# Delta rule of a DeltaNet block: the joins of six chunks in nine common steps, with the work between them placed by hand

## The chip, the cores and the metric

The kernel runs on one core of a Trainium2 chip. It is one program that issues instructions to five engines by hand: TensorE (PE in the profile, its weight loads PEld), VectorE (DVE), ScalarE (ACT), GpSimd (POOL) and SyncE (SP, which issues the weight loads from HBM). The engines wait for each other through semaphores. The metric is device time in microseconds (us) from start to end of one execution.

## The reference, cut to what matters

The block is a DeltaNet layer, an attention layer and a third layer with three attention branches and a feed-forward part. The change touches only the DeltaNet layer. There, for 16 value heads in both directions of time, tokens are cut into chunks, and each chunk needs the inverse of a triangular matrix:

```python
a = jnp.where(strict, jnp.einsum('bhncd,bhnsd->bhncs', kb, kc) * decay, 0.0)
t_inv = lax.linalg.triangular_solve(eye + a, jnp.broadcast_to(eye, a.shape),
                                    left_side=True, lower=True, unit_diagonal=True)
u = jnp.einsum('bhncs,bhnse->bhnce', t_inv, vb)
def step(s, xs):                              # the scan over chunks
    v_new = u_i - jnp.einsum('bhcd,bhde->bhce', w_i, s)
    o = jnp.einsum('bhcd,bhde->bhce', qd_i, s) + jnp.einsum('bhcs,bhse->bhce', qk_i, v_new)
    s = s * gl_i[..., None, None] + jnp.einsum('bhcd,bhce->bhde', kd_i, v_new)
...
o = rms_norm(o, o_norm_g)
return (o * jax.nn.silu(z)) @ w_out           # the gate
```

q, k and v come from a projection `u @ w_in`, a five-tap convolution over time and a silu; z from another projection. All is float32.

## The kernel before

The kernel uses 6 chunks of 128 tokens (768 in all) and goes over the 16 heads in 8 passes `j` of two heads; each pass also prepares the next one, `k = j + 1`. The order of work is one list, the generator `dn_order`. Every engine's program walks through the same list and issues its own part of each entry, in that order, so that the list sets the order on PE, DVE, ACT, POOL and SP alike. A pass has three stages:

- **Substitution.** The 16x16 diagonal blocks of all matrices go to HBM (`blocks_out`, issued by SP) and come back in another layout (`blocks_in`). DVE inverts them in 15 steps (`solve`). SP sends the inverses out and back (`inverses_out`) into `Yf`. Beside this PE runs the projection of the next pass: `proj(k, n, part)`, with `n` one of four groups of 128 columns (q, k and two v heads) and `part` one of four pieces of two contraction steps each, so 16 pieces `p[0]` to `p[15]`. When a group is done ACT copies it from PSUM to `raw`, and DVE runs its five taps (`conv(k, n, q)`). The five taps of the first group stand between the `solve` steps in DVE's queue, `conv(k, 0, 0)` behind the third step, and so the fourth step is not issued before this group is in `raw`.
- **Joins.** The inverse is put together from blocks of 16 to 32, 64 and 128 by nine steps (the table `JOINS`: x, p, y for size 16 and 32; x, w, y for 64), each on each of the six chunks. PE does 8 (sizes 16 and 32) or 4 small matmuls per chunk and step, and ACT or DVE copies each product out of PSUM before the next step of that chunk. Chunks 0 to 2 and 3 to 5 are two gangs, the second one step behind the first. Between these half steps stand larger pieces for PE: the rest of the projection, 24 pieces of the gate's projection `z`, the norms' sums (`norm`) and transposes (`turn`). The function `with_dense` cuts this list into runs, which are spread evenly over the 18 half steps.
- **Scan.** Six steps over the chunks in both directions, with the next pass's decay and Gram matrices between them. Then the outputs of both directions are summed.

The gate of pass j-1 ends in pass j: `sum_sq` (mean square, DVE and ACT), `gate_o` (two multiplications over 128x1536, DVE), `finish` (12 transposes on PE, a copy by ACT and a store). Before, `zg` (the silu of z, with two table loads on ACT, a multiplication on POOL) is the last entry ahead of the scan of its own pass.

SP's program hangs its weight loads on entries of the same list. A projection slab (2 MB, `in_w_dn`) goes to one slot of a ring of two, a gate slab (1 MB, `in_w_z`) to the other; each load waits until PE has read the slab that it replaces. SP issues in order, and a wait holds all that stands behind it:

```python
elif what == "proj" and which[1:] == [3, 3]:
    ahead += 1
    fetch(ahead)                    # the gate slab of pass k
elif what == "zg" and which[0] < 7:
    ahead += 1
    fetch(ahead)                    # the projection slab of the pass after the next
elif what == "gram" and which[1] == 1:
    blocks_out(which[0], 0, 0, 2)
elif what == "blocks":
    blocks_out(which[0], 1, 2, 6)
    blocks_in(*which)
elif what == "solved":
    inverses_out(*which)
```

`proj` waits at its part 0 for the slab. In the profile L995 and L996 are `proj`, L1032 is `z`, L1004 and L1005 `norm`, L1013 `turn`, L1074 to L1133 the join steps (L1074 x, L1084 p, L1096 y; L1109, L1121, L1133 those of size 64), L1145 to L1185 the scan, L1196 `finish`; L2283 and L2286 `conv`, L2333 and L2336 `solve`, L2412 and L2415 `gate_o` (all DVE); L1782 and L1783 `zg` (ACT); L791 `fetch`, L800 `blocks_out`, L808 `blocks_in`, L813 to L821 `inverses_out` (SP).

## Time and profile before

| | us |
|---|---|
| median of 3 runs (lowest to highest) | 3429.66 (3426.16 to 3442.43) |
| profiled execution | 3430.6 |
| its span, first to last instruction | 3428.6 |
| PE busy | 3031.3 (88%) |
| DVE busy | 1322.4 (39%) |
| ACT busy | 982.0 (29%) |

The profile is one execution. Start times count from its first instruction. A timeline row is a start time, a duration, engine, line and operation, what it writes and reads, and a count of merged instructions (a float32 matmul shows as two); in brackets stands how long the engine had been idle, and what it waited for. The joins of pass 3 begin at 663.56 us and those of pass 7 at 1282.31 us, so that a pass takes 154.7 us. The granted TensorE clock over the span is 0.961 of full speed, which is 2.4 GHz.

### The profile page before, as it was taken

The page shows a single profiled execution, that of the slowest core. Times are in us where ns is not written, and L with a number is a line of the kernel's source. Part 1 is how long each engine was busy: PE and PEld are TensorE (multiplying, and loading weights), DVE is VectorE, ACT ScalarE, POOL GpSimd, SP SyncE. Part 2 cuts the span into 40 slices and gives each one's busy share as a digit, 9 for nine tenths or more (in the row PEclk, how much of TensorE's full clock was granted, in tenths as well). Part 3 has the DMA queues.
Part 4 walks back from the last instruction along what each step waited for, and adds up shares of the span by engine and source line. Part 5 has one row for each costly group of instructions (what it writes and reads, how often), then busy time and mean ns, then how long its engine had stood idle before and what let it go on. Part 6 is the DMA issues. An engine that isn't in the chain of part 4 may idle for free.

```text
span 3428.6 us, 38158 instructions
## 1 busy us (share of the span) xinstructions
PE 3031.3 (88%) x15910; PEld 1898.8 (55%) x15910; DVE 1322.4 (39%) x2862; ACT 982.0 (29%) x2457; POOL 64.4 (2%) x52
## 2 busy tenths in 40 slices
PE   7798888888898869797999979999989989799998
PEld 3466667676666647464555433545454433388743
DVE  2346364636455453442322123322235210377601
ACT  1325435353535344001223122221124310212200
POOL 0000000000000000000000000000000000000000
PEclk9799999999999989899999999999999999899999
DMA  4101100010101011710100011111221012022211
GB/s 182 38 9 51 43 19 38 19 39 19 39 19 50 23 65 50 314 51 31 49 25 25 31 46 74 50 50 53 83 74 39 35 74 88 35 99 74 76 68 41
DMA packets 75644, 195.99 MB, mean 57 GB/s; under 512 B 56048, under 2 KB 60144, under 8 KB 64080
## 3 DMA queue, kind: packets, MB, share of 16 engines
q1 hardware_dynamic: 70064, 173.73, 14.0%
q10 hardware_dynamic: 5408, 19.83, 1.5%
q8 instruction: 125, 2.05, 0.2%
q14 instruction: 47, 0.39, 0.0%
HBM read 182.00 MB, written 11.53 MB: 56 GB/s over the span
## 4 chain that ended last, share of the span: by engine, by line
PE 75%; DVE 10%; ACT 9%; DMA 3%; issue 2%; SPq 1%; DVEq 0%
PE ps L939 12%; PE ps L1619 7%; PE ps L1032 5%; PE ps L1556 5%; PE ps L1434 5%; PE ps L1251 3%; ACT arena L1657 3%; PE ps L1566 2%; PE ps L995 2%; PE ps L1438 2%; PE ps L1318 2%; PE ps L929 2%; PE ps L1333 2%; PE ps L1252 2%; PE ps L1074 2%
## 5 line engine op out<-in xcount | busy, mean ns | idle before, releaser
L1656 ACT ACTIVATE arena<-ps 64x64 f32<-64x64 f32 (+9 forms) x952 | 314.5, 358 | 1101.2 <-PE ps L939 354.7
L939 PE MATMUL ps<-arena 128*128 128x512 f32 (+1 forms) x976 | 420.4, 590 | 46.5 <-DVE arena L2232 15.2
L939 PEld LDWEIGHTS ps<-arena 128*128 128x128 f32 x976 | 187.6, 194 | 273.5 <-issue 229.9
L995 PE MATMUL ps<-arena 128*128 128x512 f32 x512 | 265.2, 599 | 1.7 <-DVE arena L2232 1.7
L1619 PE MATMUL ps<-arena 128*128 128x256 f32 x1176 | 254.5, 378 | 0.0
L1619 PEld LDWEIGHTS ps<-arena 128*128 128x128 f32 x1176 | 222.2, 189 | 32.6 <-issue 0.5
L1032 PE MATMUL ps<-arena 128*128 128x256 f32 x768 | 205.4, 404 | 15.0 <-DVE arena L2304 8.7
L1657 ACT ACTIVATE arena<-ps,arena 128x128 f32<-128x128 f32 x544 | 158.4, 368 | 140.8 <-PE ps L1057 48.3
L1556 PE MATMUL ps<-arena 128*128 128x512 f32 x384 | 173.2, 603 | 20.3 <-issue 20.3
L1434 PE MATMUL ps<-arena 128*128 128x512 f32 x384 | 179.8, 596 | 5.1 <-ACT arena L1988 3.2
L996 PEld LDWEIGHTS ps<-arena 128*128 128x128 f32 x512 | 97.0, 189 | 124.4 <-issue 124.4
L1032 PEld LDWEIGHTS ps<-arena 128*128 128x128 f32 x768 | 138.7, 194 | 39.1 <-DVE arena L2304 9.5
L996 PE MATMUL ps<-arena 128*128 128x256 f32 x512 | 152.7, 380 | 0.0
L2551 DVE SCALAR_TENSOR_TENSOR arena<-arena 128x512 f32<-128x512 f32 x45 | 30.5, 748 | 307.7 <-ACT arena L1672 307.7
L1251 PE MATMUL ps<-arena 128*128 128x512 f32 x256 | 133.1, 601 | 16.8 <-DMA arena<-scratch 16.8
L1556 PEld LDWEIGHTS ps<-arena 128*128 128x128 f32 x384 | 73.2, 194 | 110.1 <-issue 110.1
L2286 DVE SCALAR_TENSOR_TENSOR arena<-arena 128x770 f32<-128x770 f32 x128 | 130.2, 1017 | 2.9
L1318 PEld LDWEIGHTS ps<-arena 128*128 128x128 f32 x728 | 99.9, 193 | 47.8 <-issue 20.4
L1665 ACT ACTIVATE arena<-arena 128x512 f32<-128x512 f32 (+2 forms) x61 | 37.4, 628 | 294.0 <-DVE arena L2471 195.2
L2510 DVE SCALAR_TENSOR_TENSOR arena<-ps,arena 128x128 f32<-128x128 f32 (+2 forms) x80 | 31.3, 392 | 210.1 <-PE ps L1532 139.7
L1318 PE MATMUL ps<-arena 128*128 128x128 f32 x728 | 103.5, 277 | 8.5 <-DVE arena L2520 8.4
L995 PEld LDWEIGHTS ps<-arena 128*128 128x128 f32 x512 | 95.6, 191 | 14.9 <-issue 1.8
(295 smaller groups left out, 4200.8 us busy)
## 6 DMA issues: line engine op xcount, KB each, us to landing
arena<-in_ada_w SPq DMA_DIRECT2D x12, 2048.0 KB, 17.4
arena<-in_w_up SPq DMA_DIRECT2D x11, 2048.0 KB, 7.8
arena<-in_w_dil SPq DMA_DIRECT2D x9, 2048.0 KB, 7.6
arena<-in_w_dn SPq DMA_DIRECT2D x8, 2048.0 KB, 9.7
arena<-in_w_gate SPq DMA_DIRECT2D x6, 2048.0 KB, 12.5
arena<-in_w_down SPq DMA_DIRECT2D x8, 1408.0 KB, 6.1
arena<-in_att_in SPq DMA_DIRECT2D x5, 2048.0 KB, 8.0
arena<-in_w_z SPq DMA_DIRECT2D x8, 1024.0 KB, 5.0
```

Of the source, the lines that this page charges most:

```text
L939: m = e.matmul(out, w[:, (k * m_tiles + x) * 128:(k * m_tiles + x) * 128 + 128], src(k), start=k == 0, stop=k == nk - 1)
L995: e.matmul(ps[:, b1, :], w, uT[:, k * T_ALL + 256:(k + 1) * T_ALL], start=k == 0, stop=k == 7)
L996: m = e.matmul(ps[:, b2, 0:256], w, uT[:, k * T_ALL:k * T_ALL + 256], start=k == 0, stop=k == 7)
L1032: m = e.matmul(ps[:, b, (c % 2) * 256:(c % 2) * 256 + 256], uT[:, k * T_ALL + c * 128:k * T_ALL + c * 128 + 128], wv[:, k, :], start=k == ...
L1251: e.matmul(ps[:, b, :], lhsT, s[:, 256:768], start=k == 0, stop=k == 15)
L1318: m = e.matmul(psf[:, b * 512 + c * 128:b * 512 + c * 128 + 128], P[:, c * 128:c * 128 + 128], diag[lane], start=True, stop=True)
L1434: m = e.matmul(ps[:, b, :], w[:, (4 * k + n) * 128:(4 * k + n) * 128 + 128], hk(k), start=k == 0, stop=k == 7)
L1556: m = e.matmul(ps[:, b, :], w[:, k * 512 + x * 128:k * 512 + x * 128 + 128], hk(k), start=k == 0, stop=k == 7)
L1619: m = e.matmul(ps[:, b, 0:256], left[:, k], right[:, k], start=k == 0, stop=k == 3)
L1656: return e.activation(out, x, ACT.Copy)
L1657: return e.activation(out, x, ACT.Copy, scale=scale)
L2286: e.scalar_tensor_tensor(cv[n], r[:, q:q + 770], cw[:, q:q + 1], cv[n], MUL, ADD).then_inc(*(mark("tap", j, n, q) if q < 4 else mark("conv ...
```

## The change

- The joins are no longer two gangs. Each of the nine steps is issued for all six chunks, and behind each step stands a list written by hand (`behind`).
- Each chunk has its own buffer `joined` (six per size in place of three), so `join_p` no longer waits for the `y` step of chunk c - 3. The loads that fill them at the start double from 6 to 12, 128 KB each.
- `p[14]` and the first two taps of `conv(k, 2)` move ahead of the first join step.
- `zg(j)` moves out of the joins of pass j to the substitution of pass j + 1, between `p[2]` and `p[3]`; in pass 7 it stays in the joins. `gate_o` moves from ahead of the `solve` steps to behind step 8, `finish` from behind step 7 to behind step 12.
- The PSUM banks of the projection groups are exchanged (`PROJ`).
- SP's program is not edited, but its `fetch` at `zg` moves with the entry.

```diff
--- before.py
+++ after.py
@@ -248,20 +248,6 @@
 JOINS = [(what, size) for size in (16, 32) for what in ("x", "p", "y")] + [("x", 64), ("w", 64), ("y", 64)]
 
 
-
-DENSE = ("proj", "z", "norm", "turn", "mod_k")
-
-
-def with_dense(slices):
-
-    runs = []
-    for s in slices:
-        if s[0] in DENSE or not runs:
-            runs.append([])
-        runs[-1].append(s)
-    return runs
-
-
 def dn_order():
 
 
@@ -278,6 +264,9 @@
 
     def gate(j, i, banks=(0, 1)):
         return [("z", j, c, part, banks[i % 2]) for c in (2 * i, 2 * i + 1) for part in range(4)]
+
+    def beside(one, other):
+        return [x for both in itertools.zip_longest(one, other) for x in both if x]
 
     def norms(j, n):
         return [("norm_sq", j, n), ("norm", j, n), ("norm_x", j, n), ("turn", j, n)]
@@ -311,48 +300,54 @@
             yield next(z)
     for j in range(8):
         k = j + 1
+
         if j < 7:
             p = project(k)
-
-            taps = [*conv(k, 2, 2, 5), *conv(k, 3)]
-            z = gate(j, 0) if j else []
-            rest = [p[14], *conv(k, 2, 0, 2), p[15], *(x for pair in itertools.zip_longest(taps, z) for x in pair if x),
-                    ("silu", k), ("norm_sq", k, 0), *gate(j, 1), ("norm", k, 0), ("norm_x", k, 0), ("norm_sq", k, 1),
-                    ("turn", k, 0), *gate(j, 2), ("norm", k, 1), ("norm_x", k, 1), ("turn", k, 1), ("zg", j)]
+            t = [*conv(k, 2, 2, 5), *conv(k, 3)]
+            z1, z2 = gate(j, 1), gate(j, 2)
+            if j:
+                z0 = gate(j, 0)
+                behind = [[p[15]], beside(t[:4], z0[:4]), beside(t[4:], z0[4:]), z1]
+            else:
+                behind = [[p[15]], beside(t[:4], z1[:3]), beside(t[4:], z1[3:5]), z1[5:]]
+            behind[2] += [("silu", k), ("norm_sq", k, 0)]
+            behind += [[("norm", k, 0), ("norm_x", k, 0), ("norm_sq", k, 1)], [("turn", k, 0), *z2[:3]], z2[3:],
+                       [("norm", k, 1), ("norm_x", k, 1)], [("turn", k, 1)]]
         else:
             p = [("mod_k", n, x) for n in (4, 5) for x in range(8)]
-            rest = [*p[14:], *gate(7, 0), *gate(7, 1), *gate(7, 2), ("zg", 7)]
+            z0, z1, z2 = (gate(7, i) for i in range(3))
+            behind = [[p[15]], z0[:4], z0[4:], z1[:4], z1[4:], z2[:3], z2[3:6], [*z2[6:], ("zg", 7)], []]
         yield "clean", j
         yield "blocks", j
         if j:
             yield "sum_sq", j - 1
         yield from p[:3]
         if j:
-            yield "gate_o", j - 1
+            yield "zg", j - 1
         yield p[3]
-        beside = {3: 4, 5: 5, 8: 6, 10: 7, 12: 8, 14: 9}
+        early = {3: 4, 5: 5, 8: 6, 10: 7, 12: 8, 14: 9}
         for i in range(1, 16):
             yield "solve", j, i
-            if i in beside:
-                yield p[beside[i]]
+            if i in early:
+                yield p[early[i]]
                 if j < 7 and i < 14:
-                    yield "conv", k, 0, beside[i] - 4
-            if i == 7 and j:
+                    yield "conv", k, 0, early[i] - 4
+            if i == 8 and j:
+                yield "gate_o", j - 1
+            if i == 12 and j:
                 yield "finish", j - 1
         yield "solved", j
         yield p[10]
         if j < 7:
             yield from conv(k, 1)
         yield from p[11:14]
-        runs, done = with_dense(rest), 0
-        steps = [(gang, at) for step in range(len(JOINS) + 1) for gang, at in ((range(3), step), (range(3, 6), step - 1))
-                 if 0 <= at < len(JOINS)]
-        for i, (gang, at) in enumerate(steps):
-            for c in gang:
-                yield (*JOINS[at], j, c)
-            now = len(runs) * (i + 1) // len(steps)
-            yield from itertools.chain(*runs[done:now])
-            done = now
+        if j < 7:
+            yield from conv(k, 2, 0, 2)
+        yield p[14]
+        for (what, size), more in zip(JOINS, behind):
+            for c in range(6):
+                yield what, size, j, c
+            yield from more
         also = {s: [] for s in range(6)}
         if j < 7:
             for s, c in enumerate((0, 3, 4, 2, 5)):
@@ -505,7 +500,7 @@
 
 
         Ab, XT, tmp16 = take(768), take(768), take(450)
-        joined = {size: [take(256) for _ in range(3)] for size in (16, 32)}
+        joined = {size: [take(256) for _ in range(6)] for size in (16, 32)}
         XL = [rr, vn, vd, qs, Ab[:, 0:512], Sst]
         XW = [oB[:, c * 256:c * 256 + 256] for c in range(6)]
 
@@ -677,7 +672,7 @@
             return x.rearrange("p (m f l) -> p m f l", m=4, f=4)
 
 
-        PROJ, GRAM = ((0, 1), (2, 3), (6, 7), (0, 1)), (0, 1, 1, 3, 0, 3)
+        PROJ, GRAM = ((6, 7), (0, 1), (2, 3), (0, 1)), (0, 1, 1, 3, 0, 3)
 
         LEFT = (1, 1, 5, 4, 4, 5)
 
@@ -1094,7 +1089,7 @@
                 for u in range(4):
                     for U in UPPER:
                         m = e.matmul(ps[U, b, u * 32:u * 32 + 32].rearrange("p (b t) -> p b t", t=size),
-                                     un64(joined[size][c % 3][U], u), blocks_of(quadrant(Yf, c, u, U, U), size, u % 2, 1),
+                                     un64(joined[size][c][U], u), blocks_of(quadrant(Yf, c, u, U, U), size, u % 2, 1),
                                      start=True, stop=True)
                 m.then_inc(*mark("inv_pe", j, c, "y", size))
                 leave_banks(("inv_act", j, c, "y", size), b)
@@ -1692,7 +1687,7 @@
             e.dma_start(expa, D["a_log"].partition_broadcast(128)).then_inc(*landed("in_alog"))
             e.dma_start(onorm, D["o_norm_g"].partition_broadcast(128)).then_inc(*landed("in_onorm"))
             for i, size in enumerate((16, 32)):
-                for n in range(3):
+                for n in range(6):
                     e.dma_start(joined[size][n], D["join"][i]).then_inc(*landed(f"in_joins{size}", n))
 
 
@@ -2342,12 +2337,9 @@
 
             def join_p(size, j, c):
                 e.wait_ge(*at("inv_pe", j, c, "p", size))
-                if c < 3:
-                    e.wait_ge(*at(f"in_joins{size}", 2))
-                else:
-                    e.wait_ge(*at("inv_pe", j, c - 3, "y", size))
+                e.wait_ge(*at(f"in_joins{size}", 5))
                 for d in range(2):
-                    m = e.tensor_tensor(both(joined[size][c % 3], size, d, 0), narrow(2 + c, size, d), partners(size, d), MUL)
+                    m = e.tensor_tensor(both(joined[size][c], size, d, 0), narrow(2 + c, size, d), partners(size, d), MUL)
                 m.then_inc(*mark("inv_dve", j, c, "p", size))
 
             def halves_x(j, c):
```

SyncE, from the end of one pass's inverses to those of the next (98 rows in both). Before, with L791 the weight loads, L800 `blocks_out`, L808 `blocks_in`, L813 to L821 the inverses:

```order
L821 DMA arena<-blocks 16x24x16 x8
L791 DMA arena<-in_w_z 128x2048
L791 DMA arena<-in_w_dn 128x4096
L800 DMA blocks<-arena 16x8x16 x8
L800 DMA blocks<-arena 16x16x16 x8
L808 DMA arena<-blocks 96x256 x2
L813 DMA blocks<-arena 96x256
```

In the changed kernel the same lines are numbered five lower:

```order
L816 DMA arena<-blocks 16x24x16 x8
L786 DMA arena<-in_w_z 128x2048
L795 DMA blocks<-arena 16x8x16 x8
L795 DMA blocks<-arena 16x16x16 x8
L803 DMA arena<-blocks 96x256 x2
L786 DMA arena<-in_w_dn 128x4096
L808 DMA blocks<-arena 96x256
```

The 2 MB slab `in_w_dn` now stands behind both `blocks_out` and `blocks_in`. It does so for the slabs 2 to 7, and once more for `in_ada_w` in pass 7.

TensorE, the first half of the joins of pass 1. Before:

```order
L1074 MATMUL ps<-arena 64x64 x24
L995 MATMUL ps<-arena 128x512
L996 MATMUL ps<-arena 128x256
L995 MATMUL ps<-arena 128x512
L996 MATMUL ps<-arena 128x256
L1084 MATMUL ps<-arena 64x32 x24
L995 MATMUL ps<-arena 128x512
L996 MATMUL ps<-arena 128x256
L995 MATMUL ps<-arena 128x512
L996 MATMUL ps<-arena 128x256
L1074 MATMUL ps<-arena 64x64 x24
L1032 MATMUL ps<-arena 128x256 x2
```

In the changed kernel, from the last piece ahead of the joins (L990 and L991 are `proj`, L1069, L1079 and L1091 the steps x, p and y, L1027 `z`):

```order
L991 MATMUL ps<-arena 128x256
L1069 MATMUL ps<-arena 64x64 x48
L990 MATMUL ps<-arena 128x512
L991 MATMUL ps<-arena 128x256
L990 MATMUL ps<-arena 128x512
L991 MATMUL ps<-arena 128x256
L1079 MATMUL ps<-arena 64x32 x48
L1027 MATMUL ps<-arena 128x256 x8
L1091 MATMUL ps<-arena 64x32 x48
L1027 MATMUL ps<-arena 128x256 x8
L1069 MATMUL ps<-arena 64x64 x48
L1027 MATMUL ps<-arena 128x256 x16
```

Half steps of 24 small matmuls became steps of 48, and one piece of two L995 and two L996 left the joins.

VectorE, in the substitution of pass 1, around `solve` step 8. Before:

```order
L2336 TENSOR_REDUCE arena<-arena 96x2x8
L2286 SCALAR_TENSOR_TENSOR arena<-arena 128x770
L2333 TENSOR_TENSOR arena<-arena 96x162
L2336 TENSOR_REDUCE arena<-arena 96x2x9
L2333 TENSOR_TENSOR arena<-arena 96x200
```

In the changed kernel:

```order
L2331 TENSOR_REDUCE arena<-arena 96x2x8
L2281 SCALAR_TENSOR_TENSOR arena<-arena 128x770
L2404 TENSOR_TENSOR arena<-arena 128x1536
L2407 TENSOR_TENSOR arena<-arena 128x1536
L2328 TENSOR_TENSOR arena<-arena 96x162
```

The two multiplications of `gate_o` moved from ahead of the first step to the middle of the chain of steps.

## Rows read from the trace of the kernel before

**Rows 1.** SP's issues, passes 2 and 3 (start, duration, engine, line, operation, count)

```profile
569.72 0.43 SPq L791 DMA_DIRECT2D arena<-in_w_dn  x1
603.58 27.29 SPq L800 DMA_DIRECT2D blocks<-arena  x16
632.33 0.78 SPq L808 DMA_DIRECT2D arena<-blocks  x2
654.98 0.30 SPq L813 DMA_DIRECT2D blocks<-arena  x1
```

**Rows 2.** PE's timeline, substitution of pass 3

```profile
624.60 1.02 PE L995 MATMUL ps<-arena 128*128 128x512 f32 x2
...
634.49 0.59 PE L996 MATMUL ps<-arena 128*128 128x256 f32 x2
...
640.08 1.47 PE L1196 MATMUL ps<-arena 128*128 128x128 f32 x12
...
661.60 0.59 PE L996 MATMUL ps<-arena 128*128 128x256 f32 x2
663.56 1.61 PE L1074 MATMUL ps<-arena 64*64 64x64 f32 x48 [1.36 <-DMA arena<-blocks]
```

**Rows 3.** DVE's timeline, the same stretch

```profile
635.38 1.76 DVE L2412 TENSOR_TENSOR arena<-arena 128x1536 f32<-128x1536 f32 x1 [2.69 <-ACT arena L1877]
637.25 1.76 DVE L2415 TENSOR_TENSOR arena<-arena 128x1536 f32<-128x1536 f32 x1
...
639.99 0.61 DVE L2283 TENSOR_SCALAR arena<-arena 128x770 f32<-128x770 f32 x1
...
654.33 0.62 DVE L2336 TENSOR_REDUCE arena<-arena 96x30 f32<-96x450 f32 x1
```

**Rows 4.** ACT's timeline, the same stretch

```profile
634.28 0.64 ACT L1656 ACTIVATE arena<-arena 96x256 f32<-96x256 f32 x1 [3.37 <-DMA arena<-blocks]
...
635.26 0.85 ACT L1656 ACTIVATE arena<-ps 128x512 f32<-128x512 f32 x2
```

**Rows 5.** DMA issues by line: KB each, median us from issue to landing

```profile
arena<-in_w_dil SPq DMA_DIRECT2D x9, 2048.0 KB, 7.6
arena<-in_w_dn SPq DMA_DIRECT2D x8, 2048.0 KB, 9.7
...
arena<-in_w_down SPq DMA_DIRECT2D x8, 1408.0 KB, 6.1
```

**Rows 6.** PE's timeline, first work after an idle stretch

```profile
54.23 2.04 PE L995 MATMUL ps<-arena 128*128 128x512 f32 x2 [1.70 <-DVE arena L2232]
...
1261.62 2.82 PE L1196 MATMUL ps<-arena 128*128 128x128 f32 x12 [9.08 <-DVE arena L2415]
```

**Rows 7.** busy time in the joins of pass 3 (span, engines, PEclk, DMA)

```profile
core 0: us, PE busy (x) PEld busy (x) DVE busy (x) ACT busy (x) POOL busy (x), PEclk, DMA share, GB/s
663.56:728.79 65.23, 59.49 (x852) 46.16 (x853) 19.22 (x48) 27.05 (x91) 0.00 (x0) 0.97 0.05 17
```

**Rows 8.** PE's timeline, joins and first scan step of pass 3

```profile
674.34 1.61 PE L1074 MATMUL ps<-arena 64*64 64x64 f32 x48
675.88 2.00 PE L1032 MATMUL ps<-arena 128*128 128x256 f32 x8
...
708.14 0.88 PE L1013 MATMUL ps<-arena 128*128 128x128 f32 x6 [0.99 <-ACT arena L1761]
...
711.85 1.38 PE L1032 MATMUL ps<-arena 128*128 128x256 f32 x4 [1.31 <-DVE arena L2304]
...
728.79 1.06 PE L1164 MATMUL ps<-arena 128*128 128x128 f32 x8
...
733.69 2.08 PE L1185 MATMUL ps<-arena 128*128 128x128 f32 x8 [1.40 <-ACT arena L1657]
```

**Rows 9.** ACT's timeline, start of the scan of pass 3

```profile
728.92 1.28 ACT L1782 ACT_TABLE_LOAD   x1
...
733.01 1.14 ACT L1657 ACTIVATE arena<-ps,arena 128x128 f32<-128x128 f32 x4
```

## The prediction

> **What bounds the kernel now.** I read the busy shares first: PE 88%, DVE 39%, ACT 29%. A pass is bound by PE's queue, so I went through PE's timeline of one pass and asked at each gap what it waited for. In the substitution PE has no gap: it starts the next projection at 624.60 and is at it until 662.19 (661.60 + 0.59), `finish` of 1.47 included; then it waits 1.36 for the inverses to come back [rows 2]. DVE's chain of `solve` steps runs beside it and ends at 654.95 [rows 3], 8.6 before the first join step. Both sides of this stage end within 2 us of each other, so a delay of either moves the joins. In the joins PE is busy 59.5 of 65.2 us at a granted clock of 0.97 [rows 7], with waits of about 1 us each [rows 8]. At the start of the scan PE waits 1.40 for ACT, which was busy with the table loads and the silu of `zg` [rows 8, 9].
>
> Then I read SP's queue, since the order listing shows a 2 MB load moved past other entries. Before, the slab `in_w_dn` is issued at 569.72, 55 us ahead of its use in pass 3 at 624.60, and its landing (9.7 us, behind a gate slab that shares the engines) is hidden [rows 1, 2, 5]. `blocks_out` ends at 630.87 (603.58 + 27.29) and `blocks_in` is issued from 632.33 to 633.11 [rows 1]: 8.5 us after PE has begun the projection that needs the slab.
>
> **The change part by part, for a middle pass, in the times of pass 3.**
>
> *The slab.* In the changed kernel it is issued behind `blocks_in`, at 633.1. Six slabs (2 to 7) are so placed. Nothing else held it up: its slot was free since the joins. What stands behind it on SP is only the inverses' trip at 654.98 [rows 1]. A 2 MB load that does not share the engines takes 7.6 (the median of nine); 6.1 for 1.4 MB and 9.7 for the shared one are the ends [rows 5]. I take 7.7: landing at 640.8. PE's queue has nothing else ahead of `proj` part 0, so PE stands from 624.6 to 640.8: **+16.2 us** (14.6 to 18.2).
>
> The rate can also be had from the Trainium skill, "DMA: Bandwidth & Descriptors", section "Anatomy of one DMA": 2.0 us fixed plus bytes at 436 GB/s. For 2.10 MB that is an estimate of 6.8 us, 0.9 under what I take; six slabs would cost 5 us less, 3468 in place of 3473. The rows of 7.6 decide here.
>
> *The clock.* After a long stretch of little work TensorE came back at 1.2 GHz: the first pair took 2.04 against 1.02, and after 9.08 us of idling `finish` took 2.82 against 1.47 [rows 2, 6]. Pass 3 goes straight from scan to projection and has no such start. I add **+1.5** (0 to 3).
>
> *What follows the late start.* PE: 640.8 + 1.5 + 37.6 (624.60 to 662.19) = 679.9, and `p[14]`, a fourth of the 10.3 that four pieces take (624.60 to 634.49 + 0.59 [rows 2]), makes it 682.5. DVE: `solve` 1 to 3 run early, but `conv(k, 0, 0)` behind them needs group 0 out of PSUM: 640.8 + 1.5 + 10.5 plus ACT's two copies of 0.85 [rows 4] = 653.6. From that conv to the end of the chain it was 15.0 (639.99 to 654.95), and `gate_o` now stands inside the chain, 3.6 (635.38 to 639.01) [rows 3]: 672.2, and 8.6 for the trip: 680.8. So PE is the later by 1.7 and the joins begin at 682.5, 18.9 after 663.56. Of this 2.6 is `p[14]`, which the joins no longer hold: net **+16.3**. Without the late slab `gate_o`'s move would cost nothing, as it was ahead of the chain anyway; `zg` on ACT (4.1 from table load to the next instruction [rows 9]) falls where ACT waits for PE, in either case. POOL's part of it has 14 us until `gate_o`.
>
> *The joins.* Six chunks in step leave between a copy and its use the rest of the step (1.6 per three chunks) and a piece from `behind` (2.0 to 8 us of `z` at 2.00 for two pieces [rows 8]). That can remove the 5.7 of idle time and the loss by the clock, 0.03 x 65.2 = 2.0 [rows 7]. Where two edges stay uncovered I charge a wait of about 1 us, the size of those at 708.14 and 711.85 [rows 8]: `turn(k, 0)` must be copied out by DVE before `z` may have the bank, and the last `norm` puts ACT's Ln and Exp ahead of its copies of the final step. That is 2.1. Sum: -5.7 - 2.0 + 2.1 = **-5.6** (-7.7 to 0). That work is not less is plain from the order: the same number of matmuls, in longer rows. The buffers per chunk remove a wait (chunk c - 3's `y`) which the gangs had always behind them; alone 0.
>
> *The scan.* With `zg` gone ACT's copy can come at DVE's product, not at 733.01: the wait of 1.40 goes, and the slow matmuls behind it (eight of 128x128 take 2.08 there and 1.06 at 728.79) come back in part [rows 8, 9]: **-2.0** (-3 to 0).
>
> *Passes 0 and 7.* In pass 0 the slab in question was loaded at the start, so only gains count: -5.6 - 2.0, and about 1.4 more since it has fewer pieces to cover waits with before: -9. In pass 7 the late load is wanted only in the second half of the `mod_k` pieces, while PE waits for DVE anyway (9.08 idle at 1261.62 [rows 6]), and `zg(7)` still stands ahead of the scan: -1.
>
> *The start.* Six more loads of 128 KB on ACT's queue, long before the joins use them: 0 (up to 1). The exchanged banks: group 0 now needs banks 6 and 7, which the last scan step empties before its own output step, and group 2 uses 2 and 3, which the first join step wants after `p[12]` to `p[14]`: 0.
>
> Per middle pass: 16.3 - 5.6 - 2.0 = +8.7. Six of them: +52.2. With -9 and -1 the sum is +42. Against the profiled execution of 3430.6 that is 3473; the median of the runs shown, 3429.66, lies 0.9 lower, which I ignore.
>
> **The rivals.**
>
> *A, the forecast:* 3473, own range 3455 to 3495.
>
> *B, the joins give nothing back.* ACT has 24 copies in a `y` step of six chunks and, behind the first of them, the silu of q, k and v with its own table loads; DVE has eight taps and `norm_sq` ahead of its six copies. Steps of six put a whole batch behind these where the gangs had half. For it: ACT is 27 us busy in the joins [rows 7]. Against: 3 to 8 us of `z` stand behind just these steps. Its price is 5.6 in each of seven passes (+39) on 3473: 3512, and with the slab at 9.7 us (+12) 3524.
>
> *C, a cheaper slab.* 6.1 us to landing and no slow start of PE: 3.1 less in six passes, 3454; with joins that get all 7.7 back, 3440.
>
> *D, the other side: the slab is not late.* If PE met the slab in time, only the gains would stay: -7.6 in six passes, -9 and -1, together -56, so 3375. This is decided at one point: a landing before about 627, or other work in PE's queue for 16 us. For it speaks only that SP's earlier waits might end sooner, since `blocks_out` waits for DVE's last products; against it, those products are made at the very end of the scan (SP's `blocks_out` ends at 630.87, after PE's last scan work), and the trip itself is unchanged. A part of it, in which gains reach 16.3 per middle pass, would need more than all idle time of the joins, the slow clock and the scan's wait together (5.7 + 2.0 + 3 = 10.7).
>
> **How the numbers follow.** A 0.62, B 0.20, C 0.13, D 0.03, something unseen 0.02 that leaves the time about where it is. A measurement of this kernel can tell 0.5% (17 us) from no change. A, B and most of C are slower by more than that; the lower end of C and the unseen one are "same", 0.05; D is faster, 0.03; slower 0.92. The range from 3445 to 3520 leaves out D, the low end of C and the high end of B.
>
> **What the changed profile would show.** In passes 1 to 6 the first L990 of a projection stands behind a wait of about 16 us for a DMA from `in_w_dn`, and its first rows take twice their time; in pass 0 it does not. SP's timeline has the slab right behind L803. DVE waits about 15 us for ACT between `solve` 3 and the first tap. The distance from the first join step to the first scan step falls from 65.2 to about 57, of which 2.6 is `p[14]`. The wait of L1180 in scan step 0 is gone in passes 0 to 6. If the slab's wait is under 10 us, the size of the first term is wrong; if the distance in the joins stays above 61, B holds.

## The result: 1.2% slower, as the sum had it, and the profile after

Medians of four runs each on one chip: the changed kernel 3475.74 us (3466.38 to 3477.2), the kernel before 3429.68 (3426.16 to 3442.43). The ratio is 1.0122 [1.009, 1.0153]; the forecast was 3473, slower. The profiled run of the changed kernel is its fastest: 3466.38, with a span of 3464.6, 36.0 above the span before. The rows below are from it; their line numbers are the old ones less 5 (L990 and L991 `proj`, L1027 `z`, L1069, L1079 and L1091 the join steps x, p and y).

SP's timeline in pass 3, beside [rows 1]:

```profile
628.69 3.79 SPq L795 DMA_DIRECT2D blocks<-arena  x8
633.97 0.78 SPq L803 DMA_DIRECT2D arena<-blocks  x2
634.79 0.43 SPq L786 DMA_DIRECT2D arena<-in_w_dn  x1
674.47 0.30 SPq L808 DMA_DIRECT2D blocks<-arena  x1
```

The slab is issued right behind `blocks_in`. PE's timeline from its arrival, beside [rows 2]:

```profile
642.53 2.07 PE L990 MATMUL ps<-arena 128*128 128x512 f32 x2 [16.15 <-DMA arena<-in_w_dn]
644.40 1.06 PE L991 MATMUL ps<-arena 128*128 128x256 f32 x2
645.25 1.54 PE L990 MATMUL ps<-arena 128*128 128x512 f32 x2
646.63 0.60 PE L991 MATMUL ps<-arena 128*128 128x256 f32 x2
647.06 1.02 PE L990 MATMUL ps<-arena 128*128 128x512 f32 x2
```

PE stands 16.15 us, and starts at half speed. That this is the path shows in the chain of waits from 626 to 690, where the load itself is one piece:

```profile
634.79 7.69 DMA arena<-in_w_dn
642.53 2.07 PE ps L990 x2
```

The list of waits from 300 to 1300 (total us, times, longest) has it six times:

```profile
DVE arena L2278 <- ACT arena L1651: 110.6, 6, 19.0
PEld ps L990 <- DMA arena<-in_w_dn: 97.5, 6, 16.4
PE ps L990 <- DMA arena<-in_w_dn: 96.4, 6, 16.2
```

Next, what else ran under that wait: ACT's timeline, then DVE's, beside [rows 3, 4]:

```profile
636.96 1.28 ACT L1777 ACT_TABLE_LOAD   x1
638.25 1.48 ACT L1777 ACTIVATE arena<-arena 128x1536 f32<-128x1536 f32 x1
639.75 1.28 ACT L1778 ACT_TABLE_LOAD   x1
655.00 0.87 ACT L1651 ACTIVATE arena<-ps 128x512 f32<-128x512 f32 x2 [13.96 <-PE ps L991]
```

```profile
655.91 0.62 DVE L2278 TENSOR_SCALAR arena<-arena 128x770 f32<-128x770 f32 x1 [18.15 <-ACT arena L1651]
660.98 1.75 DVE L2404 TENSOR_TENSOR arena<-arena 128x1536 f32<-128x1536 f32 x1
662.83 1.76 DVE L2407 TENSOR_TENSOR arena<-arena 128x1536 f32<-128x1536 f32 x1
673.82 0.62 DVE L2331 TENSOR_REDUCE arena<-arena 96x30 f32<-96x450 f32 x1
```

`zg` is over at 641.03 and ACT then idles for 13.96 us, and `gate_o` (L2404, L2407) stands in DVE's chain, which ends at 674.44; PE reaches the joins at 684.59, without a wait there. The joins of pass 3, beside [rows 7, 8]: first their whole stretch (length, then PE, PEld, DVE, ACT, POOL busy, PE's clock, DMA share, GB/s), then rows of PE's timeline.

```profile
684.59:738.36 53.77, 51.50 (x846) 43.55 (x845) 20.73 (x50) 25.23 (x86) 0.00 (x0) 1.00 0.06 21
```

```profile
684.59 3.01 PE L1069 MATMUL ps<-arena 64*64 64x64 f32 x96
687.53 1.12 PE L990 MATMUL ps<-arena 128*128 128x512 f32 x2
...
693.23 3.73 PE L1027 MATMUL ps<-arena 128*128 128x256 f32 x16
696.89 2.99 PE L1091 MATMUL ps<-arena 64*64 64x32 f32 x96
...
706.42 7.20 PE L1027 MATMUL ps<-arena 128*128 128x256 f32 x32
713.55 2.99 PE L1079 MATMUL ps<-arena 64*64 64x32 f32 x96
...
722.80 2.87 PE L1027 MATMUL ps<-arena 128*128 128x256 f32 x12 [1.05 <-DVE arena L2299]
725.60 1.61 PE L1104 MATMUL ps<-arena 64*64 64x64 f32 x48
727.15 4.60 PE L1027 MATMUL ps<-arena 128*128 128x256 f32 x20
...
738.36 0.68 PE L1159 MATMUL ps<-arena 128*128 128x128 f32 x4 [1.22 <-ACT arena L1651]
739.43 0.71 PE L1159 MATMUL ps<-arena 128*128 128x128 f32 x4 [0.39 <-ACT arena L1651]
...
741.19 1.05 PE L1180 MATMUL ps<-arena 128*128 128x128 f32 x8
```

65.2 us have become 53.8. The two waits left are those the forecast charged: `z` behind `turn(k, 0)` (1.05), and ACT's late copies at the edge to the scan (1.22). The wait of 1.40 at the old L1185 [rows 8] is gone.

The ledger of the two profiled runs, from the starts of these stages in all passes:

| stage | before | after | difference |
|---|---|---|---|
| wait for the slab, passes 1 to 6 | 0 | 96.4 | +96.4 |
| projection's first row to the joins, passes 1 to 6 | 235.3 | 254.7 | +19.4 (15.5 of it `p[14]`, which left the joins) |
| joins, passes 1 to 6 | 63.7 to 65.2 each | 53.8 each | -61.1 |
| joins, pass 0 | 59.1 | 46.8 | -12.3 |
| scan, passes 0 to 5 | 52.2 mean | 50.0 mean | -13.1 |
| the rest (start, scan 6 with pass 7's substitution, tail) | | | +6.7 |
| span | 3428.6 | 3464.6 | +36.0 |

The medians differ by 46, ten more. The other three runs of the changed kernel took 3475 to 3477 at a mean granted clock of 0.942 to 0.943, the profiled one 3466 at 0.945. The scan is the stage that varies most: 47.5 to 54.9 us from pass to pass, longer where the granted clock in it is 0.87 to 0.90. What makes the clock drop in some scans stays open; no term of the sum below 10 us can be read from totals alone, and I compare stages.

### The profile page after: what moved, and what is told of

Same layout as the page of the kernel before. It is cut to its first block, busy times and chain, and to the rows that moved or that the text cites. A ratio compares the mean times of both kernels' runs of the same rounds, so it can differ in the third digit from the quotient of the medians.

```text
span 3464.6 us, 38189 instructions
## 1 busy us (share of the span) xinstructions
PE 3019.5 (87%) x15910; PEld 1905.0 (55%) x15910; DVE 1326.0 (38%) x2862; ACT 981.4 (28%) x2457; POOL 64.4 (2%) x52
## 3 DMA queue, kind: packets, MB, share of 16 engines
q8 instruction: 125, 2.05, 0.2%
## 4 chain that ended last, share of the span: by engine, by line
PE 81%; DVE 7%; ACT 7%; DMA 3%; issue 1%; SPq 1%; DVEq 0%; ACTq 0%
PE ps L934 12%; PE ps L1614 7%; PE ps L990 7%; PE ps L1027 5%; PE ps L1551 5%; PE ps L1429 5%; PE ps L991 3%; PE ps L1246 3%; ACT arena L1652 3%; PE ps L1561 2%; PE ps L1433 2%; PE ps L1313 2%; PE ps L924 2%; PE ps L1328 2%; PE ps L1247 2%; PE ps L1069 1%
## 5 line engine op out<-in xcount | busy, mean ns | idle before, releaser
L1651 ACT ACTIVATE arena<-ps 64x64 f32<-64x64 f32 (+8 forms) x952 | 314.3, 359 | 1134.0 <-PE ps L934 357.2
L990 PE MATMUL ps<-arena 128*128 128x512 f32 x512 | 274.6, 618 | 98.1 <-DMA arena<-in_w_dn 96.4
L934 PEld LDWEIGHTS ps<-arena 128*128 128x128 f32 x976 | 189.2, 195 | 274.3 <-issue 230.2
L1614 PE MATMUL ps<-arena 128*128 128x256 f32 x1176 | 254.5, 378 | 0.0
L1614 PEld LDWEIGHTS ps<-arena 128*128 128x128 f32 x1176 | 222.2, 189 | 32.6 <-issue 0.5
L1551 PE MATMUL ps<-arena 128*128 128x512 f32 x384 | 173.2, 603 | 20.5 <-issue 20.5
L1027 PE MATMUL ps<-arena 128*128 128x256 f32 x768 | 181.5, 388 | 7.3 <-DVE arena L2299 7.3
L1429 PE MATMUL ps<-arena 128*128 128x512 f32 x384 | 179.8, 596 | 5.1 <-ACT arena L1983 3.2
L991 PEld LDWEIGHTS ps<-arena 128*128 128x128 f32 x512 | 99.8, 195 | 130.0 <-issue 130.0
L990 PEld LDWEIGHTS ps<-arena 128*128 128x128 f32 x512 | 98.9, 197 | 113.5 <-DMA arena<-in_w_dn 97.5
L1027 PEld LDWEIGHTS ps<-arena 128*128 128x128 f32 x768 | 142.8, 191 | 29.7 <-DVE arena L2299 9.0
L991 PE MATMUL ps<-arena 128*128 128x256 f32 x512 | 156.1, 387 | 0.0
L1246 PE MATMUL ps<-arena 128*128 128x512 f32 x256 | 132.4, 598 | 16.9 <-DMA arena<-scratch 16.9
L1551 PEld LDWEIGHTS ps<-arena 128*128 128x128 f32 x384 | 73.3, 194 | 110.1 <-issue 110.1
L1313 PEld LDWEIGHTS ps<-arena 128*128 128x128 f32 x728 | 99.6, 192 | 47.8 <-issue 20.5
```

Source lines behind the costliest of these rows:

```text
L934: m = e.matmul(out, w[:, (k * m_tiles + x) * 128:(k * m_tiles + x) * 128 + 128], src(k), start=k == 0, stop=k == nk - 1)
L990: e.matmul(ps[:, b1, :], w, uT[:, k * T_ALL + 256:(k + 1) * T_ALL], start=k == 0, stop=k == 7)
L991: m = e.matmul(ps[:, b2, 0:256], w, uT[:, k * T_ALL:k * T_ALL + 256], start=k == 0, stop=k == 7)
L1027: m = e.matmul(ps[:, b, (c % 2) * 256:(c % 2) * 256 + 256], uT[:, k * T_ALL + c * 128:k * T_ALL + c * 128 + 128], wv[:, k, :], start=k == ...
L1246: e.matmul(ps[:, b, :], lhsT, s[:, 256:768], start=k == 0, stop=k == 15)
L1313: m = e.matmul(psf[:, b * 512 + c * 128:b * 512 + c * 128 + 128], P[:, c * 128:c * 128 + 128], diag[lane], start=True, stop=True)
```

## The experiments

The theory: the late slab costs about 98 us, the joins and the scan give some 56 back. The first rival: the slab costs less than its wait shows, because something else sets the end once it is on time. Ratios are to the kernel before, run on the same chip. The rounds ran on several chips, on which the kernel before took 3429.7 to 3434.0 in the median, so that a difference between two rounds is good to some 4 us; each run's change is a few lines, mostly of the hand-written order. The names e1, e2 and so on are those that the texts on record use.

**1. The slab on time (e1).** The changed kernel, with SP's fetch behind the last join step of the pass before:

```diff
-                elif what == "zg" and which[0] < 7:
+                elif what == "y" and which[0] == 64 and which[2] == 5 and which[1] < 7:
```

> The changed kernel with one edit: SP fetches the projection slab behind the last join step, as before the change, and no longer at zg. Theory (the late slab is the whole loss): PE's wait of 16.1 us for in_w_dn at the start of the projection goes in passes 1 to 6, and with it the slow first matmuls (about 2 us). The first join step then comes at 40.2 us after the start of the projection (37.6 of PE work and p[14]), not 58.2 us after the end of the scan: 18 us less in six passes, 3476 - 108 = 3368. Rival (the joins and not the slab cost the time): within 15 us of 3476. Rival (the wait only hid another one: DVE's chain with gate_o inside it, and the trip of the inverses, end late too): the inverses come back at about 38.7 us after the start of the projection by the after trace; if this is late by more than 5 us, 3400 or more.

Measured: 3389.95 (3384.55 to 3394.93), ratio 0.9887 [0.987, 0.9903]. The sign flips, so the slab's place makes the change slower. But it is worth 86 and not the 108 expected, and 3390 misses 3368 by 22. The joins are as in the changed kernel (53.8); the substitution takes 44.3 instead of 42.5 in the mean of six passes, after a start without a wait. ACT's, DVE's and PE's timelines of pass 3 show what now comes last:

```profile
610.20 1.28 ACT L1777 ACT_TABLE_LOAD   x1
611.50 1.48 ACT L1777 ACTIVATE arena<-arena 128x1536 f32<-128x1536 f32 x1
613.00 1.28 ACT L1778 ACT_TABLE_LOAD   x1
614.29 0.87 ACT L1651 ACTIVATE arena<-ps 128x512 f32<-128x512 f32 x2
```

```profile
615.20 1.72 DVE L2278 TENSOR_SCALAR arena<-arena 128x770 f32<-128x770 f32 x1 [4.20 <-ACT arena L1651]
```

```profile
625.03 2.05 PE L1191 MATMUL ps<-arena 128*128 128x128 f32 x12 [2.23 <-DVE arena L2407]
```

`zg`'s 4.1 us stand ahead of the copy of group 0, and DVE's chain of taps and solves waits 4.20 for it. PE meets the delay at `finish` (L1191), which waits for `gate_o` in that chain: 2.1 to 3.4 us in each of the six passes, and then slow rows (2.05 for 1.47). The first tap itself takes 1.72, where it took 0.62 in the changed kernel: POOL's multiplication of `zg` runs beside it until 616.50. Under the late slab all of this was hidden.

**2. The late slab alone (e2).** The kernel before, with the fetch behind `blocks_in`:

```diff
-                elif what == "zg" and which[0] < 7:
+                elif what == "sum_sq" and which[0] < 7:
```

> The kernel before with one edit: SP fetches the projection slab at sum_sq, behind blocks_in, where the changed kernel has it. Theory: PE waits 16.1 us in six passes and comes back slow (2 us); the inverses' wait of 1.4 us is swallowed: +16.7 in six passes, 3430 + 100 = 3530. Rival (part of the wait of the changed kernel is due to its new order): a wait clearly under 16 us and a time under 3500.

Measured: 3538.81 (3530.9 to 3545.9), 1.0315 [1.0292, 1.0339], +109: a wait of 16.2 to 16.5 in six passes, 98, and a substitution 0.7 longer; the joins as before (63.7). So in the kernel before there was nothing behind which the wait could hide.

**3. `zg` back in the joins (e3)**, the slab on time (order of kernel 1):

```diff
-            yield "zg", j - 1
+            pass
...
+        if j < 7:
+            yield "zg", j
```

> e1_slab_early with zg(j) back at the end of the joins of its own pass; everything else as there. Theory: the first scan step takes 3.7 us more in passes 0 to 6 (in the traces 8.05 us from the first scan matmul to the second L1145 group before, 4.4 us in the changed kernel): e1 + 26, about 3394. Rival (the gain is given back later in the scan, whose stage is shorter by only 2.2 us on average in the changed kernel, at a lower clock): e1 + 15, about 3383. Rival (zg is hidden in either place): e1.

Measured: 3387.19, 0.9872 [0.9853, 0.9891], the same as kernel 1, where 26 more were expected. The substitution falls from 44.3 to 40.1 in each pass, which the expectation left out, and the mean scan rises from 49.9 to 54.6. So in these two kernels `zg`'s place is a zero-sum matter: 4.1 us on ACT ahead of the scan or ahead of the copy. `gate_o` stands in DVE's chain here too, and PE does not wait at `finish`: its move alone costs nothing.

**4. The gate's moves alone (e4b)**, joins as before: `zg`, `gate_o`, `finish` and the projection's banks as in the changed kernel, the slab behind the last join step. With the old banks `finish` would start in a bank in which a projection group is still being summed, so that form (e4 on record) was not timed, and the exchange of the banks is part of what is measured here.

```diff
...
-            yield "gate_o", j - 1
+            yield "zg", j - 1
...
-            if i == 7 and j:
+            if i == 8 and j:
+                yield "gate_o", j - 1
+            if i == 12 and j:
                 yield "finish", j - 1
...
-        PROJ, GRAM = ((0, 1), (2, 3), (6, 7), (0, 1)), (0, 1, 1, 3, 0, 3)
+        PROJ, GRAM = ((6, 7), (0, 1), (2, 3), (0, 1)), (0, 1, 1, 3, 0, 3)
```

> The kernel before (two gangs, three buffers) with zg, gate_o and finish at the places of the changed kernel, the slab fetched behind the last join step, and the changed kernel's banks for the projection groups, which finish at its new place needs. Theory, from e1: the substitution takes 44.1 us up to the first join step and not 39.2 (+4.9 in six passes, +29), the scan 2.4 to 4.7 less in seven passes (-17 to -33): 3426 to 3442, no gain. Rival (these moves are the gain and the joins are not): under 3410.

Measured: 3461.18 against 3433.22, 1.0077 [1.0059, 1.0095]. +28, where 3426 to 3442 had been expected: in the mean of six passes the substitution is 4.8 longer (44.1 for 39.2), the joins 1.3, and the scan 2.6 shorter. From here to kernel 1 only the joins, with `p[14]` and two taps moved ahead of them, and the buffers differ: with both set against the kernel before of their own chip -68, some 10 in each of seven passes: what the nine steps are worth. The buffers were not tried alone.

So the change divides into gate's moves +28, joins -68, late slab +86. That these sum to the measured 46 proves nothing, since each is the step from one kernel to the next; that each is of the size which its stages show does.

**5. `zg` behind the copy of group 0 (e5)** (from kernel 1): `zg` behind `p[3]`, `gate_o` behind `solve` 12, `finish` behind `solve` 14.

```diff
-        yield from p[:3]
+        yield from p[:4]
         if j:
             yield "zg", j - 1
-        yield p[3]
...
-            if i == 8 and j:
+            if i == 12 and j:
                 yield "gate_o", j - 1
-            if i == 12 and j:
+            if i == 14 and j:
                 yield "finish", j - 1
```

> e1_slab_early with zg(j-1) behind p[3] (so that ACT copies group 0 out of PSUM first), gate_o behind solve 12 and finish behind solve 14. In e1 the first join step comes 44.1 us after the start of the projection, in e3_zg_in_joins 40.1: ACT has 4.1 us of table loads and silu ahead of the copy that conv(k,0,0) waits for, and DVE's chain stands behind that. Theory: the chain ends 4.0 us earlier, PE's own 40.2 us of work sets the end again, the scan stays as short as in e1 (49.9 on average): e1 - 24, about 3366. Rival (gate_o inside DVE's chain is what is late, not zg): about e1, 3390. Rival (the silu now collides with the copy of group 1 or delays gate_o): between.

Measured: 3397.58 (3388.01 to 3398.99), 0.9886 [0.987, 0.9902]. A miss by 32: no better than kernel 1. DVE's and POOL's timelines:

```profile
616.32 0.23 DVE L2330 TENSOR_REDUCE arena<-arena 96x12 f32<-96x72 f32 x1
616.58 3.57 DVE L2327 TENSOR_TENSOR arena<-arena 96x98 f32<-96x98 f32 x1
620.19 0.25 DVE L2330 TENSOR_REDUCE arena<-arena 96x14 f32<-96x98 f32 x1
```

```profile
616.53 3.44 POOL L2800 TENSOR_TENSOR arena<-arena 128x1536 f32<-128x1536 f32 x1 [21.75 <-ACT arena L1776]
```

The wait for ACT is gone, but the `solve` product of 96x98, 0.32 us in the changed kernel, takes 3.57: until POOL's multiplication of `z` by the norm's gain ends. Then PE waits 3.11 at `finish` for `gate_o`.

**6. PE kept busy under the late slab (e7):** the changed kernel with 16 matmuls of 128x512 whose result is dropped, ahead of the wait.

```diff
+                    take_banks(b1, b2)
+                    if n == 0 and j > 1:
+                        for _ in range(16):
+                            e.matmul(ps[:, b1, :], ones, uT[:, 256:T_ALL], start=True, stop=True)
                     e.wait_ge(*here("dn", j))
-                    take_banks(b1, b2)
```

> The changed kernel with the slab late as it is, and 16 extra matmuls of 128x512 (13.8 us, results overwritten) on PE ahead of the wait for the slab, in six passes. Theory: the wait is still there, in smaller part as idle time, and the projection starts at full clock in place of 2.07 + 1.06 + 1.54 for what takes 1.02 + 0.59 + 1.02: about 2 us less in six passes, 3476 - 12 = 3464. Rival (the slow start costs nothing, DVE's chain sets the end): 3476. Rival (the granted clock later in the scan, 0.87 to 1.0, also depends on this): the mean length of the scan stage, 50.0 us, changes by more than 1 us.

**7. The same with 19 (e12).**

> The changed kernel with 19 extra matmuls ahead of the wait for the slab in place of the 16 of e7_pe_kept_busy, where PE still idled 2.6 us and the projection began at 2.08 us a pair. Theory (any idle stretch ahead of the projection brings the slow start): with PE busy until about the landing the first pair takes 1.02 and the stage to the first join step falls from 41.9 to about 40.2, 3471 - 10 = 3461. Rival (the slow start comes from something else, such as the landing slab itself): the first pair takes 2.0 again and the time is 3471.

PE's timelines, 16 fillers:

```profile
631.83 13.90 PE L988 MATMUL ps<-arena 128*128 128x512 f32 x32
648.32 2.08 PE L993 MATMUL ps<-arena 128*128 128x512 f32 x2 [2.60 <-DMA arena<-in_w_dn]
```

and 19:

```profile
628.45 16.47 PE L988 MATMUL ps<-arena 128*128 128x512 f32 x38
646.05 1.13 PE L993 MATMUL ps<-arena 128*128 128x512 f32 x2 [1.13 <-DMA arena<-in_w_dn]
```

16 are not enough: PE still idles 2.60 and starts slow; 3471.38, 1.0105 [1.009, 1.012], no gain that can be told. With 19 PE idles at most 1.13 in any of the six passes and the slow start is gone, the substitution takes 40.2 instead of 42.5, and the time is 3462.98 (3459.28 to 3470.7), 1.0087 [1.0069, 1.0105]. That interval overlaps the changed kernel's, [1.009, 1.0153], so the gain is read from the stage: the slow start costs about 2 us a pass, some 12 in all; the wait itself is the rest. Less the fillers the mean scan is 50.8 with 16 and 49.8 with 19, for 50.0, so the scan does not hang on this.

**8. The last two waits of the joins (e8)** (from kernel 5): what lies behind the steps is placed one step earlier.

```diff
-            behind += [[("norm", k, 0), ("norm_x", k, 0), ("norm_sq", k, 1)], [("turn", k, 0), *z2[:3]], z2[3:],
-                       [("norm", k, 1), ("norm_x", k, 1)], [("turn", k, 1)]]
+            behind += [[("norm", k, 0), ("norm_x", k, 0), ("norm_sq", k, 1)], [("turn", k, 0)],
+                       [("norm", k, 1), ("norm_x", k, 1)], [("turn", k, 1)], z2]
```

> e5_zg_behind_raw with another order of what stands behind the joins: turn(k,0) alone behind y 32, the second norm behind x 64, turn(k,1) behind w 64, all of z2 behind the last step. The two waits of the changed joins (1.05 for DVE's copy ahead of z2, 1.2 and 0.4 for ACT ahead of the scan) are covered. Theory: joins of 53.8 become 52 (-1.8 in seven passes, -12): about 3354. Rival (x 64 now waits for ACT's 24 copies of y 32 behind the first norm, with only 0.8 us of turn between): as e5.

Measured: 3368.15 (3367.42 to 3369.61), 0.9806 [0.9791, 0.9821], 29 faster than kernel 5 where 12 were expected, though the 3354 expected, which stood on a faster kernel 5, is missed by 14. The joins take 52.2 instead of 53.8 to 55.5, the mean scan 48.9 instead of 50.3; the spans of the two profiled runs differ by 18.4. The rest of the 29 I can't place (kernel 5's own runs spread by 11).

**9. `finish` behind `p[13]` (e9)** (from kernel 8), so that PE does not wait for `gate_o`.

> e8_norms_earlier with finish behind p[13]. In e5_zg_behind_raw PE waited 3.1 us at finish for gate_o, which DVE had issued behind solve 12. Theory: this wait goes; what is left is the later of PE's 40.2 us and DVE's chain, which in e5 ended 33.3 us after the start of the projection, plus 8.6 for the trip: 41.9. So 43 to 45 become 41.9, -2 to -3 in six passes: 3368 - 15 = 3353. Rival (finish just ahead of the joins delays the step x of chunk 2, which needs its bank): 3368.

Measured: 3370.72, 0.9818 [0.9804, 0.9832]: nothing, where 3353 was expected. PE no longer waits at `finish`, but for the inverses; DVE's chain, with the step of 3.57 still in it, is the later one. The substitution is 1.2 shorter in the mean (43.5 for 44.7) and the joins are 1.3 longer (53.5 for 52.2), since their first step now comes behind a wait and runs slow. PE's timeline at the first join step:

```profile
639.96 4.56 PE L1068 MATMUL ps<-arena 64*64 64x64 f32 x96 [2.90 <-DMA arena<-blocks]
```

**10. The gain's multiplication on DVE (e10)** (from kernel 9), inside `gate_o`, so that POOL has no part:

```diff
+                z3 = zg_.rearrange("p (c n) -> p c n", n=128)
...
+                e.tensor_tensor(z3, z3, bc(onorm, 1, [128, 12, 128]), MUL).then_inc(*mark("z", j))
...
-                e.tensor_tensor(x, x, bc(onorm, 1, [128, 12, 128]), MUL).then_inc(*mark("z", j))
+                pass
```

> e9_finish_last with POOL's multiplication of z by the norm's gain (3.4 us) issued on DVE at gate_o (1.8 us). In e5 one solve multiplication (96x98, two SBUF inputs) took 3.57 us and not 0.32, from 616.58 to 620.15, while POOL's multiplication ran from 616.53 to 619.97. Theory (DVE cannot read two SBUF operands while POOL works): DVE's chain gets 3.2 us back and pays 1.8, so PE's 40.2 us set the end or nearly: e9 - 8, about 3345, and no solve step over 1 us. Rival (the long solve step had another cause): the chain is 1.8 us longer, e9 + 11, and a long step is still there.

Measured: 3344.96 (3343.23 to 3348.56) against 3433.98, 0.9742 [0.9728, 0.9756]. DVE now has 1.75 more to do, and the kernel is 26 faster than kernel 9. The 3345 expected is met by luck: it was 8 less than a kernel 9 of 3353, and the step is 26. The step of 96x98 takes 0.32 again, the substitution is 2.9 shorter in the mean and the joins 1.3, because their first step is at full speed again; the expectation had 8 us in six passes and no price for the slow step. Its timelines, DVE first, then PE at the joins:

```profile
607.72 1.75 DVE L2405 TENSOR_TENSOR arena<-arena 128x1536 f32<-128x1536 f32 x1
609.39 1.75 DVE L2407 TENSOR_TENSOR arena<-arena 128x1536 f32<-128x1536 f32 x1
611.24 1.76 DVE L2410 TENSOR_TENSOR arena<-arena 128x1536 f32<-128x1536 f32 x1
```

```profile
625.07 0.59 PE L990 MATMUL ps<-arena 128*128 128x256 f32 x2
625.67 3.01 PE L1068 MATMUL ps<-arena 64*64 64x64 f32 x96
```

In pass 3 PE goes from projection to joins without a gap, and so it does in four of the six passes; in passes 1 and 4 it waits 1.0 and 1.3 for the inverses. The joins begin 40.1 to 41.5 us after the substitution's start. This is the best version, 2.6% faster than the kernel before.

**11. Does the slab matter as much there? (e11)** Kernel 10 with the slab again behind `zg`, which is the changed kernel's place but for `zg`'s own move.

> e10_gain_on_dve with one edit: the projection slab fetched at zg again, behind blocks_in, as in the changed kernel. Theory: where PE's own work sets the end of the substitution (40.2 us in e10), the late slab costs its whole wait and the slow start, 16.1 + 2.0 in six passes: 3345 + 108 = 3453. In the changed kernel taking it away gave only 86 since zg's 4.1 us on ACT and then DVE's chain took over. Rival (the price is 86 wherever it stands): 3431.

Measured: 3454.93 (3454.78 to 3460.17), 1.0073 [1.0048, 1.0097], +110 for 108 expected: waits of 15.9 to 16.6, a slow start, and nothing that they could hide.

**12. And `zg` ahead of the copy? (e13)** Kernel 10 with `zg` between `p[2]` and `p[3]` again.

> e10_gain_on_dve with one edit: zg(j-1) between p[2] and p[3] again, so that ACT has 4.1 us of table loads and silu ahead of the copy of group 0. Theory: DVE's chain, which waits for that copy, and with it the first join step come 4 us later in six passes: 3345 + 25 = 3370, and the stage takes about 44. Rival (in e1 it was POOL's multiplication and not ACT's silu that made the stage long): 3345.

Measured: 3391.57, 0.9882 [0.9862, 0.9902], +47 where +25 was expected. PE's timeline:

```profile
650.20 5.25 PE L1069 MATMUL ps<-arena 64*64 64x64 f32 x96 [5.51 <-DMA arena<-blocks]
```

The copy comes 4.1 later in its stage and DVE's chain ends 4.2 later. The trip of the inverses behind it takes 9.8, as in kernel 9, where kernel 10 had them back within 8.4 (in both slow cases ACT's store of `finish` falls into the trip; that this is the cause was not tested). So PE waits 5.51, and the first join step then runs at half speed (5.25 for 3.01). Substitution and joins are 5.3 and 2.4 longer in the mean of six passes: 7.7 in six is 46. The slow step and the longer trip are what I had left out. The rival, that POOL's multiplication and not ACT's silu made kernel 1's stage long, falls: POOL has no part here.

## Why the prediction was right, and where it was not

**The slab: right, and shown.** Forecast +16.2 a pass, measured 16.1. Landing took 7.69 for a forecast of 7.7. The 6.8 that I had estimated from the Trainium skill, "DMA: Bandwidth & Descriptors", section "Anatomy of one DMA", is not borne out; that section gives its formula for DMAs which GpSimd issues, which I had not said, and these are issued by SP. That the wait is the cause of the slowdown is shown by kernels 1, 2 and 11, which move it alone in three surroundings. Rival D, the slab in time, is refuted by [16.15] in PE's row. Rival C's slab (6.1, no slow start) is refuted too, though the joins did come near its -7.7.

**The slow start: right in kind, 2.0 for 1.5.** From 642.53 to 647.06 four rows take 4.53 that take 2.58 at the full clock (648.35 less 647.06, twice). Kernel 7 takes it away.

**What follows the late start: PE the later side, right.** The first join step of pass 3 comes 19.2 later in its own stage, for 18.9: 58.2 (626.38 to 684.59, with the wait) against 38.96; 19.3 in the mean of six passes. DVE's wait ahead of the first tap was 18.15 for "about 15", which PE's being later hides.

**The failed sentence** is "Without the late slab `gate_o`'s move would cost nothing ..., `zg` on ACT ... falls where ACT waits for PE, in either case". The first profile does not contradict it, since there the wait for the slab covers both. The half on `gate_o` holds: with `zg` in the joins the substitution takes 40.1, PE's own work, with `gate_o` in the chain (kernel 3). The half on `zg` fails. Kernel 4 shows that without the slab's cover the moves, banks included, cost 28, and kernel 1 has the row: ACT's copy of group 0 is ready to run when `zg` is in front of it, and neither DVE nor PE at `finish` has slack behind it. "POOL's part of it has 14 us until `gate_o`" looks at when its result is wanted only; kernels 5 and 10 show that it holds up DVE meanwhile. I had asked when ACT is idle, not what it will be asked for next. It left the forecast of this kernel untouched, but made the slab look 98 dear (rival D at 3375) where it is 86 (3390).

**The joins: right in the idle time, wrong in the rest.** Forecast -5.6 net of `p[14]`, measured -7.6 (61.1 less 15.5, over six), at the end of its range. I took 5.7 of idle time and 2.0 of clock, less 2.1 of new waits. The comparison is best made with pass 2 of the kernel before, whose joins ran at full clock:

```profile
509.63:573.33 63.70, 57.96 (x852) 45.08 (x853) 19.21 (x48) 26.96 (x91) 0.00 (x0) 1.00 0.05 18
```

It is as long as four others of that kernel though its clock is 1.00, so the clock accounts for the difference between 63.7 and 65.2 only. Of the 9.9 us between 63.70 and 53.77, 2.6 is `p[14]`, 3.5 is idle time (5.74 less 2.27, both stretch less PE busy), for a forecast of 5.7 less 2.1, and 3.9 is PE's busy time for the same matmuls. "That work is not less is plain from the order" was wrong, then, and the 2.0 of clock was there to gain in one pass of six only; that the two errors go opposite ways is luck. The 3.9 fits the count of runs of one tile shape, 64x64 or 128x128: 36 in the old joins and 18 in the new. From start to start 16 matmuls of `z` take 3.66 (693.23) and 32 take 7.13 (706.42): 1.73 for eight, but eight alone took 1.93 (675.88 to 677.81 before), 0.20 more; 96 of 64x64 take 2.94 and 48 take 1.55 (725.60), so each run of them carries 0.16 as well. 18 runs fewer at 0.16 to 0.20 are 2.9 to 3.6 of the 3.9. No run varied the changes of shape alone, so this is read from rows and not shown by experiment. Rival B, joins that give nothing back, falls by the distance of 53.8.

**The scan: the size right, -2.2 for -2.0.** The wait of 1.40 went from L1185 to the first scan step as 1.22 and 0.39. Kernel 3 shows that `zg`'s leaving is worth up to 4.7 here. A mean of six stages which differ by 5 us among themselves does not settle 0.2; it agrees and no more.

**Passes 0 and 7.** Pass 0 gave 12.3 in the joins and 3.6 in its scan for a forecast of 9. From the scan of pass 6 to the end of pass 7's joins it is 3.7 longer, where -1 was forecast: PE waits 9.30 for the late `in_ada_w` at 1294.36, most of which the wait for the inverses gives back (6.69 for 10.34), and `zg(7)`, which ACT now has ahead of its copies of the last join step, makes the first scan step wait 5.06. What the middle passes gave beyond the forecast, and pass 0, outweigh it: the profiled run has +36 for the sum's +42, and the median +46. That the median comes within 3 us of 3473 is partly luck: the other three runs are about 10 slower than the profiled one, at a lower clock that nothing here explains.

## What to carry to other kernels

When a change reorders work, read every queue it passes through, the loads' above all: here one 2 MB load moved behind `blocks_out` and `blocks_in` on SP, and the 86 us that this cost outweighed the 68 that the joins gave; giving the load a trigger of its own got them back. An engine that idles is no free place for work: ask which instruction is queued behind it, and whether that one's result has slack. A large wait hides such errors, so look for them again with the wait removed.

## What the hardware showed beyond that

- DVE's product with both inputs in SBUF stood for the whole of POOL's multiplication: 3.57 us for 0.32, and again 3.57 in kernel 9 at the same step. In kernel 1 the first tap, which reads one array of SBUF, took 1.72 for 0.62 beside the same multiplication. In kernel 3 the same multiplication (3.44) ran in the scan, where DVE had almost nothing to do beside it: one copy out of PSUM, 0.76 as without it. The Trainium skill, "SBUF — State Buffer", section "Who interferes with whom", has this: an exclusive lock held for the whole instruction, for a DVE operation with two SBUF inputs against a GpSimd operation that reads SBUF. The trace agrees, by 3.57 beside 3.44. Two engines were slower than one: 1.75 more on DVE took 3.44 off POOL and gained 26 us.
- PE came back at half speed after idling 2.60 us (2.08 for a pair that takes 1.02), 2.90 (4.56 for 3.02) and 5.51 (5.25), but not after 1.13 (1.13). So a wait of 2.6 to 2.9 us on the path cost 4.3 to 4.5. The length of the wait alone does not decide: in the joins of the kernel before the same wait of 1.31 for the same DVE row was followed by rows at full speed in pass 2 (0.92 and 2.00 from 558.99, granted clock 1.00) and by slow ones in pass 3 (1.55 and 2.66 from 713.16, granted clock 0.79).
- By the rows above, a run of one tile shape on PE costs 0.16 to 0.20 us on top of its matmuls; no run shows it by experiment. The Trainium skill, "TensorEngine Tiling (Array Packing)", section "Key Properties", says that a change of tiling mode drains the engine, without a figure; the rows are in keeping with it.
